# The first map's maximum of the next step moved ahead of this step's combination, in the differential-attention heads

## The chip, the cores and the metric

The kernel runs on one NeuronCore of a Trainium2 chip. The metric is the device time of one launch in microseconds. The engines named below are PE (TensorE, the matrix engine; PEld is its loading of weights), DVE (VectorE), ACT (ScalarE), POOL (GpSimd) and SP (the engine that issues most of the DMA). Each works through its own list of instructions in the order in which the program gives them, and they meet only at semaphores.

## What is computed

One layer of a streaming encoder runs for 512 prompt rows, 16 learned meta rows and 64 sample rows with a cache: a combined projection, two groups of attention heads, an output projection, and then a retrieval of single-row experts (PEER), which takes most of the time. The change touches only the first group of heads, A: four heads of differential attention. A head has two maps of scores over the same keys. Each map gets a softmax, and the second is subtracted with a factor lambda before the product with the values:

```python
s = jnp.einsum('bqhmd,bkhmd->bhmqk', q, kk).astype(jnp.float32) * (HEAD_DIM ** -0.5)
mask = (chunk_index(k_pos)[None, :] <= chunk_index(q_pos)[:, None]) & k_valid[None, :]
p = jax.nn.softmax(jnp.where(mask, s, NEG_BIG), axis=-1)
w = p[:, :, 0] - lam * p[:, :, 1]
return jnp.einsum('bhqk,bkhe->bqhe', w.astype(v.dtype), v)
```

Queries see all chunks of 64 keys up to their own, so a block of 128 queries needs fewer keys the earlier it stands.

## The kernel before

The A heads run between about 314 and 400 us of the execution, after the eight B heads and ahead of the head norms and the output projection. Nothing else runs on PE, ACT and DVE in that stretch, and POOL is idle. The work is cut into 20 steps, five for each of the four heads: four blocks of 128 prompt queries against 144, 272, 400 and 528 keys, then one block of 64 sample queries against 592 keys. The steps are named here by that width. A step does the following, and each part has a place in the list of its engine:

- PE, `a_scores` (L782 to L797): the scores of both maps. Map m (0 or 1) goes to its own pair of PSUM banks, 0 and 1 for the first map, 2 and 3 for the second. There is one set of them only, so the scores of a map wait until ACT has taken the exponentials of that map of the step before (L786). `a_s` counts them.
- DVE, `a_greatest` (L1458 to L1475): for each map a memset that masks a corner of the scores (L1468, L1469, L1471; none in the 592 step), the row maximum (L1472) and its negative times the scale (L1475, `a_neg`).
- ACT (L1094 to L1120): the exponential of each map with that number as bias, written to `p_a` with the row sums beside it (L1104, `a_prob`). Behind the two exponentials of step s stand the copy of the outputs of step s-2 (L1112) and the copies of the transposed weights of step s-1 to `wt_a` (L1118 and L1120).
- DVE, the combination (L1482 to L1490): when both maps of the step have come, two reciprocals of the sums (L1483), the product with lambda (L1484), and the two passes that give `w_a` (L1488 and L1489, `a_w`).
- PE, `a_transpose` (L799 to L809): the weights of the step, transposed tile by tile to banks 4 and 5 (L806 and L808). It waits for `a_w` of the step and for the copies of the step before.
- PE, `a_values` (L811 to L825): the product with the values (L824), once ACT has copied the transposed weights out.

PE's order is written out by hand: in iteration n it issues the scores of step n+1, then the values of step n-1, then the transposes of step n. So the scores of step n+1 stand behind the transposes of step n-1, and behind the values of step n-2. DVE's order is: both maxima of step 0; then for each step its combination, and behind it both maxima of the next step. The tile `stat` holds the maxima, the biases, the row sums and the reciprocals of one step, in columns 0 to 8 of 16.

Of the kernel before, what the change touches and what calls it, by code (L numbers as in the profile page):

```python
# [11 lines left out]
ALU = mybir.AluOpType  # L12
ACT = mybir.ActivationFunctionType
AX_X = mybir.AxisListType.X

P = 128
# [10 lines left out]
CHUNK = 64  # L27
EPS = 1e-6
LAM_INIT = 0.2
SCALE = HD ** -0.5  # L30
NEG = -1e30
# [121 lines left out]
NA = 5 * AH  # L153
# [11 lines left out]
def bass_hybrid_step(nc, x_t, consts, tables, gains, lam_p, cache_k, cache_v, cache_vt, w_tiles, sub_keys,  # L165
# [5 lines left out]
    with ExitStack() as ctx:  # L171
        base = [16512]

        def at(name, shape, dt, off):
            return nc.alloc_sbuf_tensor_at(name, shape, dt, offset=off)

        def fixed(name, shape, dt=F32):
            n = 4 * int(np.prod(shape[1:]))
            n = (n + 31) // 32 * 32
            off = base[0]  # L180
            base[0] += n
            return at(name, shape, dt, off)

        def sem(name):
            return ctx.enter_context(nc.semaphore(name))
# [6 lines left out]
        lam = fixed("lam", [P, 8])  # L192
        lam_in = fixed("lam_in", [P, 256])

        ones_r, tri_r, ident_r, negm_r = (fixed(n, [P, P], F32R) for n in ("ones_r", "tri_r", "ident_r", "negm_r"))
        stat = fixed("stat", [P, 16])
        rs_keep = fixed("rs_keep", [P, 8])
        raw_off = base[0]
        raw = fixed("raw", [P, 2, KC, P])
# [50 lines left out]
        p_a = at("p_a", [P, 4, T], F32, m0_off)  # L250
        w_a = at("w_a", [P, 2, T], F32, m0_off + 16 * T)
# [71 lines left out]
                  for k, o in enumerate((sc_off + 24576, sc_off + 30720, norm_off + 6 * T * 4 + 4608))]  # L323
# [7 lines left out]
        psf = ps[:].rearrange("p b n -> p (b n)")  # L331
# [17 lines left out]
                     for n, no in (("n1", "x"), ("nm", "added"), ("n2", "rs"))}  # L349
# [10 lines left out]
        a_s, a_max, a_neg, a_prob = sem("a_s"), sem("a_max"), sem("a_neg"), sem("a_prob")  # L360
        a_step, a_w, a_t, a_wt, a_o, a_out = (sem("a_step"), sem("a_w"), sem("a_t"), sem("a_wt"), sem("a_o"),
                                              sem("a_out"))
# [28 lines left out]
        MULT, ADD, SUB = ALU.mult, ALU.add, ALU.subtract  # L391
# [149 lines left out]
        def _(pool):  # L541
# [34 lines left out]
            for s, (table, blk, k) in enumerate(OPS):  # L576
                if s == 0:
                    pool.wait_ge(idx_ready, 1)
                if s == N_UA:
                    pool.wait_ge(idx_ready, 2)  # L580
                slot, _, before = ring_slots[s]
                if before is not None:
                    pool.wait_ge(gath_used, before + 1)
                if before is None and slot >= RING_U:
                    pool.wait_ge(u_done, N_EXP)
                idx = idx_b[:, k:k + 1] if blk else idx_a[:, k:k + 1]
                pool.indirect_dma_start(ring[slot][:], None, u_rows if table == "u" else v_rows,  # L587
                                        bass.IndirectOffsetOnAxis(ap=idx, axis=0)).then_inc(gath_in[slot], 16)
# [400 lines left out]
        def _(act):  # L989
# [38 lines left out]
            for m, o, n in ((P, 0, 4), (T - 4 * P, 4, 1)):  # L1028
                nc.scalar.activation(nrs1[0:m, o:o + n], ps[0:m, 4, o:o + n], ACT.Sqrt, bias=eps[0:m],
                                     scale=1.0 / D).then_inc(n1["std"], 1)  # L1030
            for n in range(2, N_QKV + 1):
# [9 lines left out]
                for h in range(2):  # L1041
                    for i in vt_after(n - 1, h):
                        kt, s = VT_GROUPS[i]
                        act.wait_ge(vt_done, i + 1)
                        rows = 128 if kt < 4 else 80
# [50 lines left out]
            for s in range(NA + 2):  # L1096
                if s < NA:
                    i = s % 5
                    rows, w = (P, 144 + P * i) if i < 4 else (64, T)
                    for m in range(2):  # L1100
                        act.wait_ge(a_neg, 2 * s + m + 1)
                        if s >= 2:
                            act.wait_ge(a_w, s - 1)
                        nc.scalar.activation(p_a[0:rows, 2 * (s % 2) + m, 0:w], psf[0:rows, 1024 * m:1024 * m + w],  # L1104
                                             ACT.Exp, bias=stat[0:rows, 2 + m:3 + m], scale=SCALE,
                                             accum_out=stat[0:rows, 4 + m:5 + m]).then_inc(a_prob, 1)
                if s >= 2:
                    h, i = (s - 2) // 5, (s - 2) % 5
                    rows = A_SHAPE[i][0]
                    q0 = N_META + P * i if i < 4 else KP  # L1110
                    act.wait_ge(a_o, s - 1)
                    nc.scalar.copy(qkv[:, 8 + h, q0:q0 + rows], ps[:, 6 + s % 2, 0:rows]).then_inc(a_out, 1)  # L1112
                if 1 <= s <= NA:
                    rows, full, part = A_SHAPE[(s - 1) % 5]
                    act.wait_ge(a_t, s)
                    if s >= 3:
                        act.wait_ge(a_o, s - 2)
                    nc.scalar.copy(wt_a[:, (s - 1) % 2, 0:full, 0:rows],  # L1118
                                   ps[:, 4, 0:full * rows].rearrange("p (k q) -> p k q", q=rows))
                    nc.scalar.copy(wt_a[0:part, (s - 1) % 2, full, 0:rows], ps[0:part, 5, 0:rows]).then_inc(a_wt, 1)  # L1120
# [11 lines left out]
            m = TQ - 4 * P  # L1132
# [28 lines left out]
            for u in range(N_PQ):  # L1161
                n = B_PQ + u
                hi_part(n + 1, (u + 1) % 2, (n + 1) // 2 + 1)
                for h in range(2):
# [4 lines left out]
                    if h == 0 and u == 0:  # L1169
                        act.wait_ge(norm_sems["n2"]["sum"], 1)  # L1170
                        nc.scalar.activation(nrs[:, 0:5], ps[:, 4, 0:5], ACT.Sqrt, bias=eps,
                                             scale=1.0 / D).then_inc(norm_sems["n2"]["std"], 1)
# [108 lines left out]
            for n, (b, m) in enumerate(FIN):  # L1281
                act.wait_ge(y_sum, n + 1)
                nc.scalar.activation(sq_out[0:m], h_fin[0:m, b], ACT.Square,
                                     accum_out=ss[0:m, n:n + 1]).then_inc(y_sq, 1)
                act.wait_ge(y_sq, n + 1)
                nc.scalar.activation(ss[0:m, 8 + n:9 + n], ss[0:m, n:n + 1], ACT.Sqrt, bias=eps[0:m],
                                     scale=1.0 / D).then_inc(y_std, 1)
# [3 lines left out]
        def _(dve):  # L1291
            TT, TS = nc.vector.tensor_tensor, nc.vector.tensor_scalar
# [159 lines left out]
            def a_step_done(ins):  # L1452
                nonlocal k_step
                ins.then_inc(a_step, 1)
                k_step += 1
                dve.wait_ge(a_step, k_step)

            def a_greatest(idx):  # L1458

                i = idx % 5  # L1460
                rows, w = (P, 144 + P * i) if i < 4 else (64, T)
                for m in range(2):
                    dve.wait_ge(a_s, 2 * idx + m + 1)
                    if i < 4:

                        e0 = 1024 * m + w
                        if w > 512 and w - CHUNK < 512:
                            nc.vector.memset(psf[0:CHUNK, e0 - CHUNK:1024 * m + 512], NEG)  # L1468
                            a_step_done(nc.vector.memset(psf[0:CHUNK, 1024 * m + 512:e0], NEG))  # L1469
                        else:  # L1470
                            a_step_done(nc.vector.memset(psf[0:CHUNK, e0 - CHUNK:e0], NEG))  # L1471
                    nc.vector.tensor_reduce(stat[0:rows, m:m + 1], psf[0:rows, 1024 * m:1024 * m + w], AX_X,  # L1472
                                            ALU.max).then_inc(a_max, 1)
                    dve.wait_ge(a_max, 2 * idx + m + 1)
                    TS(stat[0:rows, 2 + m:3 + m], stat[0:rows, m:m + 1], -SCALE, None, MULT).then_inc(a_neg, 1)  # L1475

            a_greatest(0)
            for idx in range(NA):
                i = idx % 5
                rows, w = (P, 144 + P * i) if i < 4 else (64, T)  # L1480
                p0 = 2 * (idx % 2)
                dve.wait_ge(a_prob, 2 * idx + 2)  # L1482
                a_step_done(nc.vector.reciprocal(stat[0:rows, 6:8], stat[0:rows, 4:6]))  # L1483
                TT(stat[0:rows, 8:9], stat[0:rows, 7:8], lam[0:rows, 5:6], MULT).then_inc(a_step, 1)  # L1484
                k_step += 1
                if idx >= 2:
                    dve.wait_ge(a_t, idx - 1)
                a_step_done(TS(w_a[0:rows, idx % 2, 0:w], p_a[0:rows, p0, 0:w], stat[0:rows, 6:7], None, MULT))  # L1488
                nc.vector.scalar_tensor_tensor(w_a[0:rows, idx % 2, 0:w], p_a[0:rows, p0 + 1, 0:w], stat[0:rows, 8:9],  # L1489
                                               w_a[0:rows, idx % 2, 0:w], MULT, ADD).then_inc(a_w, 1)  # L1490
                if idx + 1 < NA:
                    a_greatest(idx + 1)

            dve.wait_ge(a_t, 5 * AH)
            dve.wait_ge(a_o, 5 * AH)
# [233 lines left out]
            for i in range(N_EXP):  # L1729
# [9 lines left out]
                for _ in range(along(STEP_LINE, i), along(STEP_LINE, i + 1)):  # L1739
                    s = next(steps)  # L1740
# [173 lines left out]
```

## Time and profile before

| quantity | value |
| --- | --- |
| median of three runs | 1907.2 us (1906.71 to 1913.32) |
| the profiled execution's own time | 1903.46 us |
| its span in the trace | 1901.7 us |
| mean granted clock of PE, as a share of 2.4 GHz | 0.964 |
| busy over the span: PE, DVE, ACT, POOL | 95%, 75%, 40%, 34% |
| stretch of the A heads, first maximum to last combination | 315.05 to 396.4 us |

The page cuts the span in 40 slices of 47.5 us; the A heads lie in the seventh and eighth. The shares of busy time are means over all stages, and say little of one that is 4% of the span. A row of the timeline gives the start in the span, the time it took, the engine, the line and the operation, output and inputs with their sizes, and in brackets how long the engine had been idle and what ended that. Two PE instructions stand for each fp32 product, and the time of one reaches past the start of the next, so the distance between starts is the better measure on PE. The granted clock has two levels in these rows, 1.00 (2.4 GHz) and 0.50 (1.2 GHz).

### The profile page before, as it was taken

The numbers are of one execution on the slowest core, as the hardware profiler recorded it, in microseconds if no ns is written. First come the engines' busy times: TensorE is split into PE (matmuls) and PEld (weight loads), VectorE is DVE, ScalarE is ACT, GpSimd is POOL, SyncE is SP. The second block draws the span as 40 slices with busy tenths as digits, with TensorE's granted clock in tenths as the row PEclk, the third lists the DMA queues.
The fourth block names the chain that finished last, engine by engine and source line by source line (L and its number), as shares of the span: only waits on it lengthen the run. The fifth ranks groups of instructions, "written<-read, shape, count | busy, mean of one in ns | idle before, by whom it ended". The sixth has DMA issues, their size and how long they took to land.

```text
span 1901.7 us, 26560 instructions
## 1 busy us (share of the span) xinstructions
PE 1802.8 (95%) x9787; PEld 1543.1 (81%) x9787; DVE 1435.7 (75%) x2752; ACT 769.7 (40%) x1535; POOL 645.4 (34%) x409
## 2 busy tenths in 40 slices
PE   6999999999999889999899999978999999999997
PEld 6999666579999889999899999967766766766764
DVE  4433675735678788989999999858687788797787
ACT  4122564543444433433667788512222222222222
POOL 1200000000000033434233356545475566575662
PEclk9999898859999999999999999989999999999998
DMA  6243100002221589999788899999999999999996
GB/s 215 71 147 106 34 1 1 1 3 67 68 78 59 180 309 330 323 306 328 259 280 297 283 380 387 386 403 372 401 375 387 402 397 385 400 382 390 400 380 219
DMA packets 156480, 484.52 MB, mean 255 GB/s; under 512 B 15216, under 2 KB 56176, under 8 KB 152768
## 3 DMA queue, kind: packets, MB, share of 16 engines
q1 hardware_dynamic: 98992, 270.92, 39.1%
q0 software_dynamic: 56928, 208.28, 29.9%
q10 hardware_dynamic: 432, 3.64, 0.5%
q8 instruction: 78, 1.28, 0.3%
q14 instruction: 50, 0.41, 0.1%
HBM read 422.61 MB, written 59.90 MB: 254 GB/s over the span
## 4 chain that ended last, share of the span: by engine, by line
PE 66%; DVE 16%; DMA 12%; issue 3%; ACT 2%; SPq 0%; DVEq 0%; ACTq 0%
PE ps L973 16%; PE ps L951 15%; PE ps L607 10%; DMA g_in<-gates_scattered 7%; PE ps L982 5%; PE ps L888 5%; DVE hot L1690 3%; DVE w_lo L1296 3%; PE ps L708 3%; DMA raw<-w_tiles 2%; DVE ring L1709 2%; PE ps L939 2%; PE ps L699 2%; PE ps L751 2%; PE ps L795 1%
## 5 line engine op out<-in xcount | busy, mean ns | idle before, releaser
L951 PE MATMUL ps<-md_hi,w_hi 128*128 128x384 f32 x1024 | 360.8, 352 | 39.1 <-DVE w_lo L1296 39.0
L951 PE MATMUL ps<-md_hi,w_lo 128*128 128x384 f32 x1024 | 348.0, 340 | 0.0
L951 PE MATMUL ps<-md_lo,w_hi 128*128 128x384 f32 x1024 | 347.9, 340 | 0.0
L587 POOL DMA_INDIRECT ring<-u_rows,idx_a x128 | 197.0, 1539 | 402.6 <-DVE dots L1709 294.7
L1296 DVE TENSOR_TENSOR w_lo<-raw,w_hi 128x1024 fp32r<-128x1024 f32 x176 | 215.2, 1223 | 88.3 <-ACT w_hi L1226 68.0
L587 POOL DMA_INDIRECT ring<-v_rows,idx_a x128 | 223.8, 1749 | 139.1 <-DVE acc L1717 107.8
L1709 DVE CUSTOM_DVE_ANT_0 ring<-ring,x_n 128x1024 f32<-128x1024 f32 x192 | 230.3, 1221 | 10.6 <-DMA ring<-u_rows,idx_b 8.8
L951 PEld LDWEIGHTS ps<-md_hi,w_hi 128*128 128x128 f32 x1024 | 196.3, 192 | 47.2 <-DVE w_lo L1296 46.5
L1717 DVE SCALAR_TENSOR_TENSOR acc<-ring,actg,acc 128x1024 f32<-128x1024 f32 x188 | 234.1, 1277 | 0.0
L973 PE MATMUL ps<-w_hi,p_hi 128*128 128x512 f32 x576 | 192.0, 415 | 10.5 <-DVE w_lo L1773 10.3
L951 PEld LDWEIGHTS ps<-md_lo,w_hi 128*128 128x128 f32 x1024 | 196.4, 192 | 0.0
L951 PEld LDWEIGHTS ps<-md_hi,w_lo 128*128 128x128 f32 x1024 | 195.6, 191 | 0.0
L973 PE MATMUL ps<-w_hi,p_lo 128*128 128x512 f32 x576 | 182.3, 397 | 0.0
L973 PE MATMUL ps<-w_lo,p_hi 128*128 128x512 f32 x576 | 180.6, 395 | 0.0
L1265 ACT CAST w_hi<-v_buf 128x1024 fp32r<-128x1024 f32 x96 | 100.4, 1046 | 189.0 <-PE ps L973 176.4
L1773 DVE TENSOR_TENSOR w_lo<-v_buf,w_hi 128x1024 fp32r<-128x1024 f32 x96 | 117.1, 1220 | 77.8 <-ACT w_hi L1265 77.7
L607 PE MATMUL ps<-m_hi,w_hi 128*128 128x296 f32 (+1 forms) x512 | 157.0, 307 | 15.6 <-DVE w_lo L1296 14.8
L982 PE MATMUL ps<-v_buf,act_in 128*128 128x512 f32 x384 | 170.0, 592 | 0.0
L607 PE MATMUL ps<-m_hi,w_lo 128*128 128x296 f32 (+1 forms) x512 | 154.0, 301 | 0.0
L607 PE MATMUL ps<-m_lo,w_hi 128*128 128x296 f32 (+1 forms) x512 | 153.6, 300 | 0.0
L973 PEld LDWEIGHTS ps<-w_hi,p_hi 128*128 128x128 f32 x576 | 107.6, 189 | 52.9 <-issue 29.5
L1226 ACT CAST w_hi<-raw 128x1024 fp32r<-128x1024 f32 x127 | 132.4, 1042 | 35.6 <-DMA raw<-w_tiles 35.6
(254 smaller groups left out, 3269.8 us busy)
## 6 DMA issues: line engine op xcount, KB each, us to landing
raw<-w_tiles SPq DMA_DIRECT2D x176, 512.0 KB, 5.5
v_buf<-v_rows SPq DMA_DIRECT2D x128, 512.0 KB, 12.6
activated<-act_st SPq DMA_DIRECT2D x128, 192.0 KB, 4.7
gates_scattered<-g_st SPq DMA_DIRECT2D x24, 1024.0 KB, 6.4
g_in<-gates_scattered SPq DMA_DIRECT2D x32, 768.0 KB, 16.8
act_in<-activated SPq DMA_DIRECT2D x32, 768.0 KB, 13.7
kv_t<-qkv ACTq DMA_DIRECT2D x3, 1184.0 KB, 4.8
xh<-x_t SPq DMA_DIRECT2D x8, 296.0 KB, 6.2
```

The source lines that it names most:

```text
L587: pool.indirect_dma_start(ring[slot][:], None, u_rows if table == "u" else v_rows, bass.IndirectOffsetOnAxis(ap=idx, axis=0)).then_inc(gat ...
L607: mm = nc.tensor.matmul(ps[:, 2 * slot + h, 0:width], w[:, slot, kc, :], x[:, kc, c0:c0 + width], start=(m == 0), stop=(m == 23))
L888: mm = nc.tensor.matmul(ps[:, 2 * slot + h, 0:HQ], w[:, slot, kc, :], x[:, kc, h * HQ:(h + 1) * HQ], start=(kc == 0 and j == 0), stop=(kc ...
L951: mm = nc.tensor.matmul(ps[:, slot, 0:ND], w[:, slot, kc, :], x[:, kc, :], start=(kc == 0 and j == 0), stop=(kc == KC - 1 and j == 2))
L973: mm = nc.tensor.matmul(ps[:, 2 + 2 * t + h, :], p[:, q % 3, t * P:(t + 1) * P], v[q % 2][:, 512 * h:512 * h + 512], start=(i == 0 and n = ...
L982: mm = nc.tensor.matmul(ps[:, 2 + 2 * t + h, :], act_in[i // 4 % 3][:, i % 4, t * P:(t + 1) * P], v_buf[i % V_SLOTS][:, 512 * h:512 * h + ...
L1226: nc.scalar.copy(w_hi[:, n % 2], raw_u[k]).then_inc(hi_ready, 1)
L1265: nc.scalar.copy(v_hi[q % 2], v_buf[i % V_SLOTS][:]).then_inc(v_hi_ready, 1)
L1296: TT(w_lo[:, slot], raw[:, slot] if src is None else src, w_hi[:, slot].bitcast(F32), SUB).then_inc(w_split, 1)
L1709: nc.vector.tensor_tensor_reduce(rows, rows, x_n[:, blk], 1.0, 0.0, MULT, ADD, dots[:, blk, k:k + 1]).then_inc(gath_used, 1)
L1717: nc.vector.scalar_tensor_tensor(dst, rows, by, dst, MULT, ADD).then_inc(gath_used, 1)
L1773: TT(v_lo[q % 2], v_buf[i % V_SLOTS][:], v_hi[q % 2].bitcast(F32), SUB).then_inc(v_ready, 1)
```

## The change

DVE's `a_greatest` takes one map instead of both. In the new order the first map's maximum of step n+1 stands ahead of the combination of step n, and the second map's behind it. Since the numbers of step n are still needed when those of step n+1 are written, `stat` gets 32 columns, and step n uses columns 16 * (n % 2) onwards; ACT reads the bias and writes the sums there. No instruction is added or removed, no size is changed, and PE's order and ACT's order stay as they were.

```diff
-        stat = fixed("stat", [P, 16])
+        stat = fixed("stat", [P, 32])
...
+                    z = 16 * (s % 2)
...
-                                             ACT.Exp, bias=stat[0:rows, 2 + m:3 + m], scale=SCALE,
-                                             accum_out=stat[0:rows, 4 + m:5 + m]).then_inc(a_prob, 1)
+                                             ACT.Exp, bias=stat[0:rows, z + 2 + m:z + 3 + m], scale=SCALE,
+                                             accum_out=stat[0:rows, z + 4 + m:z + 5 + m]).then_inc(a_prob, 1)
...
-            def a_greatest(idx):
+            def a_greatest(idx, m):
...
-                for m in range(2):
-                    dve.wait_ge(a_s, 2 * idx + m + 1)
+                z = 16 * (idx % 2)
+                dve.wait_ge(a_s, 2 * idx + m + 1)
...
-            a_greatest(0)
+            a_greatest(0, 0)
+            a_greatest(0, 1)
             for idx in range(NA):
+                if idx + 1 < NA:
+                    a_greatest(idx + 1, 0)
...
                 dve.wait_ge(a_prob, 2 * idx + 2)
...
                 if idx + 1 < NA:
-                    a_greatest(idx + 1)
+                    a_greatest(idx + 1, 1)
```

## Rows read from the trace of the kernel before

**Rows 1.** The page: its span, and the engines of the chain that ended last.

```profile
span 1901.7 us, 26560 instructions
...
PE 66%; DVE 16%; DMA 12%; issue 3%; ACT 2%; SPq 0%; DVEq 0%; ACTq 0%
```

**Rows 2.** Stretches of the A heads: length; busy PE, PEld, DVE, ACT, POOL; granted clock; DMA.

```profile
315.05:396.40 81.35, 75.29 (x318) 46.38 (x319) 57.17 (x200) 38.44 (x136) 0.00 (x0) 0.75 0.00 1
317.70:331.36 13.66, 12.77 (x39) 7.18 (x39) 9.08 (x33) 5.74 (x20) 0.00 (x0) 0.50 0.01 2
331.36:345.01 13.65, 12.38 (x67) 7.81 (x65) 10.00 (x37) 7.38 (x28) 0.00 (x0) 1.00 0.00 0
345.01:351.84 6.83, 6.83 (x24) 3.91 (x23) 4.60 (x15) 2.39 (x8) 0.00 (x0) 0.50 0.00 0
351.84:365.50 13.66, 12.42 (x65) 7.76 (x65) 10.03 (x38) 7.41 (x28) 0.00 (x0) 1.00 0.01 1
365.50:372.32 6.82, 6.82 (x26) 4.29 (x25) 4.95 (x16) 2.41 (x8) 0.00 (x0) 0.50 0.00 1
...
379.14:392.80 13.66, 13.66 (x46) 8.14 (x45) 9.09 (x31) 5.84 (x21) 0.00 (x0) 0.50 0.01 2
```

**Rows 3.** Waits in 315 to 400 us: who for whom, total us, times, longest.

```profile
DVE stat L1483 <- ACT p_a L1104: 14.8, 20, 0.9
...
DVE stat L1472 <- PE ps L795: 3.0, 4, 1.1
DVE ps L1468 <- PE ps L795: 2.4, 2, 1.2
```

**Rows 4.** One head, 355.89 to 375.66 us: stretch, then DVE's groups by line.

```profile
355.89:375.66 19.77, 18.69 (x87) 11.67 (x86) 14.30 (x51) 9.77 (x35) 0.00 (x0) 0.83 0.01 1
...
L1472 DVE TENSOR_REDUCE stat<-ps 128x1 f32<-128x144 f32 (+4 forms) x10 | 5.6, 558 | 1.0 <-PE ps L795 0.8
...
L1483 DVE RECIPROCAL stat<-stat 128x2 f32<-128x2 f32 (+1 forms) x5 | 0.8, 164 | 3.7 <-ACT p_a L1104 3.7
```

**Rows 5.** Timeline of DVE: the maxima of steps 144 and 592.

```profile
355.89 0.11 DVE L1471 MEMSET ps<- 64x64 f32 x1
...
356.54 0.11 DVE L1471 MEMSET ps<- 64x64 f32 x1
...
371.29 0.77 DVE L1472 TENSOR_REDUCE stat<-ps 64x1 f32<-64x592 f32 x1 [0.77 <-PE ps L795]
...
372.16 0.76 DVE L1472 TENSOR_REDUCE stat<-ps 64x1 f32<-64x592 f32 x1
```

**Rows 6.** Timeline of PE at clock 1.00: first-map scores, and transposes of step 528.

```profile
357.10 0.72 PE L795 MATMUL ps<-qkv 64*128 64x272 f32 x2
...
360.13 0.94 PE L795 MATMUL ps<-qkv 64*128 64x400 f32 x2 [0.19 <-ACT p_a L1104]
...
372.99 0.42 PEld L806 LDWEIGHTS ps<-cst,w_a 128*128 128x128 f32 x4
...
373.69 0.51 PE L795 MATMUL ps<-qkv 64*128 64x144 f32 x2
```

**Rows 7.** Timeline at clock 0.50: scores of 528, transposes of 400, scores of 592.

```profile
384.58 2.33 PE L795 MATMUL ps<-qkv 64*128 64x512 f32 x8
...
388.70 0.50 PEld L806 LDWEIGHTS ps<-cst,w_a 128*128 128x128 f32 x3 [0.22 <-issue]
...
389.75 0.18 PEld L795 LDWEIGHTS ps<-k_cache,qkv 64*64 64x64 f32 x1 [0.42 <-issue]
...
392.02 0.77 DVE L1472 TENSOR_REDUCE stat<-ps 64x1 f32<-64x592 f32 x1 [0.52 <-PE ps L795]
```

**Rows 8.** Timeline: values of step 528 and the transposes behind them; ACT's first copy.

```profile
355.03 1.38 PEld L824 LDWEIGHTS ps<-wt_a,v_nat 128*128 128x128 f32 x10 [0.48 <-ACT wt_a L1120]
...
356.53 0.20 PEld L806 LDWEIGHTS ps<-cst,w_a 64*128 64x128 f32 x2
...
374.02 0.58 ACT L1118 COPY wt_a<-ps 128x512 f32<-128x512 f32 x1
```

More of the change, by code:

```diff
@@ L1456, in a_step_done @@
                 dve.wait_ge(a_step, k_step)
-            def a_greatest(idx):
+            def a_greatest(idx, m):
                 i = idx % 5
                 rows, w = (P, 144 + P * i) if i < 4 else (64, T)
-                for m in range(2):
-                    dve.wait_ge(a_s, 2 * idx + m + 1)
[L1464 to L1475, printed above, removed]
@@ L1477, in _ @@
-            a_greatest(0)
+                z = 16 * (idx % 2)
+                dve.wait_ge(a_s, 2 * idx + m + 1)
+                if i < 4:
+                    e0 = 1024 * m + w
+                    if w > 512 and w - CHUNK < 512:
+                        nc.vector.memset(psf[0:CHUNK, e0 - CHUNK:1024 * m + 512], NEG)
+                        a_step_done(nc.vector.memset(psf[0:CHUNK, 1024 * m + 512:e0], NEG))
+                    else:
+                        a_step_done(nc.vector.memset(psf[0:CHUNK, e0 - CHUNK:e0], NEG))
@@ L1478, in _ @@
+                nc.vector.tensor_reduce(stat[0:rows, z + m:z + m + 1], psf[0:rows, 1024 * m:1024 * m + w], AX_X,
+                                        ALU.max).then_inc(a_max, 1)
+                dve.wait_ge(a_max, 2 * idx + m + 1)
+                TS(stat[0:rows, z + 2 + m:z + 3 + m], stat[0:rows, z + m:z + m + 1], -SCALE, None, MULT).then_inc(a_neg, 1)
+            a_greatest(0, 0)
+            a_greatest(0, 1)
             for idx in range(NA):
+                if idx + 1 < NA:
+                    a_greatest(idx + 1, 0)
@@ L1479, in _ @@
                 i = idx % 5
                 rows, w = (P, 144 + P * i) if i < 4 else (64, T)
-                p0 = 2 * (idx % 2)
+                p0, z = 2 * (idx % 2), 16 * (idx % 2)
                 dve.wait_ge(a_prob, 2 * idx + 2)
-                a_step_done(nc.vector.reciprocal(stat[0:rows, 6:8], stat[0:rows, 4:6]))
-                TT(stat[0:rows, 8:9], stat[0:rows, 7:8], lam[0:rows, 5:6], MULT).then_inc(a_step, 1)
+                a_step_done(nc.vector.reciprocal(stat[0:rows, z + 6:z + 8], stat[0:rows, z + 4:z + 6]))
@@ L1485, in _ @@
+                TT(stat[0:rows, z + 8:z + 9], stat[0:rows, z + 7:z + 8], lam[0:rows, 5:6], MULT).then_inc(a_step, 1)
                 k_step += 1
@@ L1487, in _ @@
                     dve.wait_ge(a_t, idx - 1)
-                a_step_done(TS(w_a[0:rows, idx % 2, 0:w], p_a[0:rows, p0, 0:w], stat[0:rows, 6:7], None, MULT))
-                nc.vector.scalar_tensor_tensor(w_a[0:rows, idx % 2, 0:w], p_a[0:rows, p0 + 1, 0:w], stat[0:rows, 8:9],
+                a_step_done(TS(w_a[0:rows, idx % 2, 0:w], p_a[0:rows, p0, 0:w], stat[0:rows, z + 6:z + 7], None, MULT))
+                nc.vector.scalar_tensor_tensor(w_a[0:rows, idx % 2, 0:w], p_a[0:rows, p0 + 1, 0:w], stat[0:rows, z + 8:z + 9],
                                                w_a[0:rows, idx % 2, 0:w], MULT, ADD).then_inc(a_w, 1)
                 if idx + 1 < NA:
-                    a_greatest(idx + 1)
+                    a_greatest(idx + 1, 1)
             dve.wait_ge(a_t, 5 * AH)
```

## The prediction

> **What bounds the kernel now.** I read the page first: the chain that ended last lies 66% on PE and 16% on DVE [rows 1], but that is a mean over the whole kernel. So the second view is the table of stretches of the A heads [rows 2], the third who waited for whom there [rows 3], the fourth DVE's groups in one head [rows 4]. The stage from first maximum to last combination takes 81.35 us. Two things are to be seen. DVE is busy 57.2 of 81.35 us. And PE is at its lower clock level, 0.50 (1.2 GHz), in four stretches: 13.66 + 6.83 + 6.82 + 13.66 = 41.0 us, half of the stage; outside them it is at 1.00 (2.4 GHz) [rows 2]. DVE waits 14.8 us, in 20 waits, for the exponentials (one at each combination) and 3.0 + 2.4 = 5.4 us, in 6 waits, for scores [rows 3]; the first of these two is what the change aims at. Every wait of the second kind that I found lies where the clock is 0.50 or was so when the scores were made; the two in rows here (0.77 and 0.52 us) do [rows 5, 7].
>
> So DVE bounds the stage nearly alone. A head is a loop of five steps on DVE: both maxima, the wait for the second exponential, the combination. Head three shows it: 19.77 us, of which 3.7 wait for exponentials and 0.8 for scores; the other 15.27 are work with its hand-offs (14.30 busy) [rows 4]. In this I need the maxima apart. From the start of one map's maximum to the start of the next map's it is 0.65 us at 144 keys (355.89 to 356.54) and 0.87 at 592 (371.29 to 372.16) [rows 5], the first and last of five; the three between read the same way give 0.78, 0.91 and 1.05, longest at 528, which has two memsets. One map of a head costs 0.65 + 0.78 + 0.91 + 1.05 + 0.87 = 4.26 us, the combinations 15.27 - 2 x 4.26 = 6.75.
>
> **The change, part by part.** No instruction comes or goes and no size changes, and no DMA issue is moved; SP and POOL have nothing in this part of their lists that hangs on it. The wider `stat` costs 64 bytes a partition and no time. The second set of columns takes away a dependency only. Both are costed at nothing, with no cover needed.
>
> What is left is the order on DVE. Before, from the end of one combination to the start of the next, DVE does maximum, maximum, wait for an exponential. Per head that is 2 x 4.26 + 3.7 = 12.2, plus score waits. After, it does the second maximum of step n, then the first maximum of step n+1, and only then the combination of n. The exponential of the second map now runs beside that first maximum: 0.65 to 1.05 us of cover for waits of 14.8 / 20 = 0.74 on average. That wait goes, nearly whole: 3.7 us a head.
>
> The price: the moved maximum waits for `a_s` of step n+1, and the combination of step n is queued behind that wait, with the copies, the values and the transposes that hang on it. In PE's list the first-map scores of step n+1 stand behind the transposes of step n-1, which wait for the combination of n-1. Before, this path had the whole of two maxima and an exponential to hide in. Now DVE's loop goes through it: end of combination n-1, transposes of n-1, first-map scores of n+1, first maximum of n+1, combination of n. In each step DVE's time between combination n-1 and the moved maximum is the larger of one maximum and the PE path. What the change trades, per head, is
>
> - gone: one map's maxima from the line between combinations, 4.26, and the exposed exponentials, 3.7: 7.96 us at either clock; and the score waits, 5.4 / 4 = 1.35 on average;
> - in: the PE path, five times.
>
> The path at clock 1.00. Transposes to scores: 0.70 for five tiles (372.99 to 373.69); four loads took 0.42, so 0.105 a tile and 0.17 after the last [rows 6]. By that the transposes of 144, 272, 400, 528 take 0.38, 0.49, 0.59, 0.70, and those of 592, five half-size tiles, I put at 0.48: sum 2.64. First-map scores: 0.51 for 144 keys, 0.72 for 272, 0.94 for 400 [rows 6]; with 0.04 to reach DVE 0.55, 0.76, 0.98. The wider ones don't stand alone in the trace at this clock; I take half of the clock-0.50 durations below plus a fixed 0.1: 1.27 and 1.24. Sum 4.80. Hand-offs from DVE to PE: 5 x 0.04 = 0.2. Once a head PE comes late to the transposes: at the 592 step the values of 528 take 1.50 (355.03 to 356.53) [rows 8] and start only when ACT has done its second exponential and the copies; laid out along the new order they end 0.5 after the combination. Sum 2.64 + 4.80 + 0.2 + 0.5 = 8.1 us. Against 7.96 that is even: a head of 15.27 - 4.26 + 8.1 = 19.1 us, where one without score waits took 15.27 + 3.7 = 18.97.
>
> The path at clock 0.50. Four tiles and the gap behind them take 1.05 (388.70 to 389.75); first-map scores of 592 reach DVE after 2.27 (389.75 to 392.02); those of 528 take 2.33 from 384.58, both maps side by side, so one is hardly shorter [rows 7]. Scaled by tiles and by keys: transposes 0.63, 0.83, 1.05, 1.27, 0.79, sum 4.6; scores 0.90, 1.32, 1.75, 2.34, 2.28, sum 8.6. With 0.2 of hand-offs and PE late by 0.9 in two or three places, 14.3 us. A head: 11.0 + 14.3 = 25.3 us. The heads before, half at this level, took 20.3 each on average (81.35 / 4).
>
> These are the ends, 8.1 and 14.3; the share of each clock decides between them. I take the share that the stage has now, one half of the time: heads per us are 0.5 / 19.1 + 0.5 / 25.3, so a head takes 21.8 us and four take 87.1. That is 87.1 - 81.35 = 5.7 us more. The gain (3.7 a head) is there and is used up, because work that hid under DVE's loop is now a link of it. What is late next is PE: the transposes and scores.
>
> A rule of the Trainium skill speaks to that share. The rows show PE's clock rising behind stretches in which it never stood still: at 351.84 behind 6.83 us in which PE was busy for 6.83, at 372.32 behind 6.82 of 6.82 [rows 2]. "TensorE: Matmul & The Clock Gate", part 1, says that the throttled state is the default and that activity releases it, and the trace agrees. Taken strictly, a stage in which PE's waits get shorter would keep the higher level, which is the third rival below; by the share of now it is the sum above.
>
> **The sum.** The profiled execution took 1903.46 us, span 1901.7; with 5.7 more it would take 1909.2. The median of the three runs, 1907.2, is 3.7 above that execution, so I add the same 5.7 to it: 1912.9, given as 1913.
>
> **Rivals.**
> 1. The low clock holds longer. PE has more to wait for in each loop at 0.50, and if the level sticks, DVE's loop is PE's: slower. For: the two long low stretches (13.66 us) show that it can stay for more than half a head [rows 2]. Against: at 0.50 the new loop keeps PE almost without a gap, after which it rose each time. At a share of 65% four heads take 4 / (0.35 / 19.1 + 0.65 / 25.3) = 90.8, 9.5 over now; all low is 101.2, 19.9 over. From about 65% on it decides: 1917 to 1927 us.
> 2. The path is hidden after all: PE gets the scores done under the second maximum, or my chain has a link that isn't there. Then DVE loses only its waits for exponentials, 14.8 us, and keeps the 5.4 for scores: 1907.2 - 14.8 = 1892.4. Against: PE's written order leaves no way for scores n+1 to pass transposes n-1, and even at 1.00 the path of every step (1.3 us or more) is longer than a maximum (0.65 to 1.05).
> 3. The clock stays at 1.00 nearly throughout. Four heads of 19.1 are 76.4, 4.9 less than now: 1902.3; with up to a third of the time low, up to 1909. For: the rule above. Against: the stage has fallen back to 0.50 four times while PE was busy 12.4 of 13.65 us [rows 2], and the new order doesn't make it much denser.
> 4. The change does nothing, because the order makes no difference. It can't be quite so: DVE takes its list in order, so the combination does stand behind the new wait. A net of zero is possible, inside case 3.
>
> **How the numbers follow.** Forecast 0.67 (share of the low clock a third to 65%; 1909 to 1917), rival 1 0.17 (1917 to 1927), rival 3 with 4 0.13 (1902 to 1909), rival 2 0.03. The likeliest is 1913. The range reaches over most of rival 3 and the nearer half of rival 1, leaving out rival 2 and the far ends: 1903 to 1921. 0.5%, about what a measurement of this kernel can tell from no change, is 9.5 us: faster means under 1897.7, slower above 1916.7. Faster 0.03 (rival 2); slower 0.20 (rival 1 and the edge of the forecast); within 0.77.
>
> **What the profile of the changed kernel would show.** The waits of L1483 for exponentials fall from 14.8 us to under 2. DVE's waits for L795 rise from 5.4 us to 20 or more, in nearly all of 19 steps, and are longest ahead of the maxima of 528 and 592. The chain in this stretch alternates L806, L795, L1472, L1489. Busy times of DVE and ACT stay. A head takes about 19 us where the clock is 1.00 and 24 to 25 where it is 0.50. The prediction is wrong if L1472's waits for L795 stay near 5 us (rival 2), or if the low level holds for well over or under half of the stage (rivals 1 and 3).

## The result, and the profile after

| quantity | before | after |
| --- | --- | --- |
| median | 1907.72 us (12 runs, 1898.06 to 1917.91) | 1921.65 us (12 runs, 1917.36 to 1931.96) |
| ratio | | 1.0074, 95% interval 1.0053 to 1.0096 |
| profiled execution: own time, span | 1903.46, 1901.7 us | 1919.99, 1918.2 us |
| A heads, first maximum to last combination | 315.05 to 396.4, 81.35 us | 317.0 to 414.4, 97.4 us |

The change is slower by 14 us, 0.74%. In the profiled executions it is 16.5 us of span, and 16.1 of them lie in the A heads; from the last combination to the end it is 1505.3 us before and 1503.8 after. So the place is settled without an experiment: the rest of the kernel is as it was, within 2 us on either side.

A single execution of either kernel can still differ from another by more than the change does. One source lies ahead of the A heads, in a part that no run here touches: in the profiled executions the A heads start between 314.9 us and 327.1 us. In the three that start at 326 us or later (the experiments e1, e6 and e8 below) the clock was low for longer in the B heads. The stretch from 200 to 250 us, in the kernel before (mean clock 0.83) and in e6 (0.56):

```profile
200.00:250.00 50.00, 48.77 (x265) 35.48 (x266) 36.02 (x91) 30.64 (x72) 0.00 (x0) 0.83 0.00 1
200.00:250.00 50.00, 49.19 (x189) 34.74 (x189) 26.48 (x66) 22.69 (x54) 0.00 (x0) 0.56 0.00 1
```

So the length of the A heads, read from a profile, says more about this change than one execution's total does.

The stretches of the A heads after the change (as [rows 2]: length; busy PE, PEld, DVE, ACT, POOL; granted clock; DMA). The first block is the page's span. In the second block the first line is the stage, the second its longest stretch at one clock level, the third one head.

```profile
span 1918.2 us, 26560 instructions
```

```profile
317.00:414.40 97.40, 93.44 (x315) 59.99 (x316) 55.34 (x199) 38.40 (x136) 0.00 (x0) 0.53 0.00 1
319.80:391.50 71.70, 70.19 (x234) 45.70 (x234) 39.65 (x143) 28.11 (x99) 0.00 (x0) 0.50 0.00 1
344.72:370.03 25.31, 24.94 (x87) 16.47 (x86) 13.84 (x52) 9.80 (x36) 0.00 (x0) 0.50 0.00 1
```

DVE's busy time is nearly what it was (57.2 and 55.3 us; in the rows below each reciprocal starts while the small instruction ahead of it still runs, 349.12 against 349.05 + 0.15), and so is ACT's. What changed is the clock: 0.53 on average over the stage, against 0.75 in [rows 2]. A mean of 0.53 from two levels means 94% of the time at 0.50. PE shows busy 70.19 of 71.70 us in the low stretch, and the level did not rise within it.

Who waited for whom on DVE, 317 to 415 us (us in total, times, longest), against [rows 3]. The lines of the changed kernel are numbered a little differently: the reciprocal is L1487, a map's masking starts at L1469 or L1472, and its maximum is L1473.

```profile
DVE ps L1472 <- PE ps L795: 17.9, 11, 2.1
DVE stat L1473 <- PE ps L795: 9.8, 4, 2.5
DVE ps L1469 <- PE ps L795: 9.5, 4, 2.4
DVE stat L1487 <- ACT p_a L1105: 0.9, 1, 0.9
```

The waits for exponentials are gone, 14.8 us down to 0.9, the one that is left being that of the last step. In their place stand 37.2 us of waits for scores, in 19 waits, one for each moved maximum, where there were 5.4 us in 6. The timeline of DVE over one step shows the new order:

```profile
349.05 0.15 DVE L1476 TENSOR_SCALAR stat<-stat 128x1 f32<-128x1 f32 x1
349.12 0.16 DVE L1487 RECIPROCAL stat<-stat 128x2 f32<-128x2 f32 x1
...
349.78 0.50 DVE L1493 SCALAR_TENSOR_TENSOR w_a<-p_a,stat,w_a 128x272 f32<-128x272 f32 x1
350.29 0.11 DVE L1472 MEMSET ps<- 64x64 f32 x1
...
351.04 0.15 DVE L1476 TENSOR_SCALAR stat<-stat 128x1 f32<-128x1 f32 x1
353.56 0.10 DVE L1469 MEMSET ps<- 64x48 f32 x1 [2.37 <-PE ps L795]
```

The combination of the 272 step runs without a wait (349.12), then comes the second maximum of the 400 step (350.29), and then DVE stands 2.37 us for the first-map scores of the 528 step. Over the five steps of this head the waits are 2.13, 2.37, 2.46, 1.79 and 1.73 us. The chain of waits shows what they wait for (start, length, what):

```profile
349.78 0.51 DVE w_a L1493
350.30 0.04 issue
350.34 0.69 PE ps L806 x2
351.03 0.21 PE ps L808
351.24 2.24 PE ps L795 x5
353.48 0.36 issue
353.84 0.45 PE ps L795 x2
354.28 1.87 PE ps L824 x6
356.15 0.83 PE ps L806 x3
356.99 0.21 PE ps L808
357.20 2.16 PE ps L795 x5
```

From the end of a combination it goes to the transposes and to the scores, as the new loop has it; and on the wide steps it doesn't come back to DVE at all, but runs through scores, values (L824) and transposes on PE alone. At this clock PE is the bound for most of the head. The rows of PE say the same: in four of the five steps the transposes start 0.2 to 0.57 us after the combination is done, because PE is still at the values of the step before; only at the 272 step (done at 350.28, started at 350.34) is PE ready.

### The profile page after: what moved, and what is told of

Same layout as the page of the kernel before. It is cut to its first block, busy times and chain, and to the rows that moved or that the text cites. A ratio compares the mean times of both kernels' runs of the same rounds, so it can differ in the third digit from the quotient of the medians.

```text
span 1918.2 us, 26560 instructions
## 1 busy us (share of the span) xinstructions
PE 1824.1 (95%) x9787; PEld 1558.5 (81%) x9787; DVE 1434.5 (75%) x2752; ACT 770.2 (40%) x1535; POOL 645.4 (34%) x409
## 4 chain that ended last, share of the span: by engine, by line
PE 72%; DVE 16%; DMA 7%; ACT 3%; issue 2%; SPq 0%; DVEq 0%; ACTq 0%
PE ps L973 18%; PE ps L951 16%; PE ps L607 10%; PE ps L982 7%; PE ps L888 5%; DMA g_in<-gates_scattered 3%; DVE w_lo L1297 3%; DVE hot L1694 3%; PE ps L708 3%; DVE ring L1713 2%; DMA raw<-w_tiles 2%; PE ps L939 2%; PE ps L795 2%; PE ps L824 2%; PE ps L699 2%
```

## The experiments

Two theories stood after the result. One: the new order costs what the sum says, and the excess over 5.7 us is the clock, which stayed at 0.50. The other: something else of the change costs (the wider tile), or the path is longer than summed even at clock 1.00. Medians and ratios are over all executions, the ratios against runs of the kernel before on the same chip. The last two columns are each from the one profiled execution of the run; "low" is the share of clock 0.50 in the A heads of the run's profile, worked out from the granted clock as in the section above.

| run | median us | ratio, 95% interval | A heads us | low |
| --- | --- | --- | --- | --- |
| the changed kernel | 1921.65 | 1.0074 (1.0053 to 1.0096) | 97.4 | 94% |
| e1_stat_only | 1904.69 | 0.9987 (0.9964 to 1.0011) | 81.8 | 58% |
| e2_scores_ahead | 1943.64 | 1.0182 (1.0119 to 1.0245) | 116.4 | 97% |
| e3_scores_ahead_old_dve | 1945.47 | 1.0188 (1.0136 to 1.024) | 117.2 | 98% |
| e5_start_together | 1933.0 | 1.0138 (1.0078 to 1.0198) | 103.8 | 90% |
| e6_after_fill | 1912.88 | 1.0039 (1.0005 to 1.0073) | 85.2 | 12% |
| e7_before_fill | 1903.57 | 0.9987 (0.9958 to 1.0015) | 78.5 | 13% |
| e8_ahead_fill | 1982.06 | 1.0375 (1.0323 to 1.0427) | 148.3 | 98% |
| e9_after_fill_early | 1919.42 | 1.0078 (1.0051 to 1.0105) | 98.9 | 72% |
| e10_only_144_fill | 1930.14 | 1.0135 (1.0108 to 1.0163) | 93.9 | 73% |
| e11_before_fill_early | 1911.29 | 1.0013 (0.9989 to 1.0036) | 82.6 | 43% |
| e12_before_fill_again | 1905.05 | 0.9989 (0.997 to 1.0008) | 78.4 | 13% |
| e4_after_again (one execution) | 1919.63 | | 94.7 | 86% |

**The wider tile alone.** DVE's old order in the changed kernel:

```diff
             for idx in range(NA):
-                if idx + 1 < NA:
-                    a_greatest(idx + 1, 0)
...
                 if idx + 1 < NA:
+                    a_greatest(idx + 1, 0)
                     a_greatest(idx + 1, 1)
```

> The changed kernel with DVE's old order put back: both maxima of the next step behind the combination. What stays of the change is the wider stat with its two sets of columns. Theory (the new order costs the time, through the path transposes, first-map scores, first maximum): like the kernel before, ratio 0.997 to 1.003, DVE's waits for L795 about 5 us in the A heads, for exponentials about 15. Rival (the wider tile, which moves every later tile by 64 bytes, or the alternating columns, cost something): a good part of the 14 us stays, ratio 1.004 or more.

It measures as the kernel before, 0.9987 with an interval around 1. Its A heads:

```profile
326.10:407.90 81.80, 76.87 (x318) 48.48 (x319) 57.07 (x199) 38.39 (x136) 0.00 (x0) 0.71 0.00 1
```

81.8 us at a mean clock of 0.71. The tile costs nothing that can be measured here; the 14 us are the order. The share of the low clock is 58% in this profile and was 50% in the kernel before, with the same order of work: it moves by that much between two executions.

**First-map scores ahead of the transposes.** If the loop through the transposes is the cost, it can be cut in PE's list:

```diff
             a_scores(0)
+            a_scores(1, (0,))
             for idx in range(NA + 1):
                 if idx + 1 < NA:
-                    a_scores(idx + 1)
+                    a_scores(idx + 1, (1,))
                 if idx >= 1:
                     a_values(idx - 1)
+                if idx + 2 < NA:
+                    a_scores(idx + 2, (0,))
```

e2 has it on the changed kernel, e3 on the kernel before.

> The changed kernel with PE's list changed too: the first-map scores of step n+2 stand ahead of the transposes of step n (and behind the values of n-1), so that the moved maximum no longer waits for transposes. Theory: the loop through the combination, the transposes and the scores is cut; DVE's waits for L795 fall well under the changed kernel's. At clock 1.00 a head should take about 17.5 us instead of 19.1, the stage about 73 us, 8 less than before: 1900 us. At clock 0.50 the two maps' scores no longer run side by side and PE alone needs about 30 us a head, so a stage that stays low would take up to 120 us and the kernel would be slower than the changed one, 1935 or more. Rival (the moved maximum itself, not its wait on PE's order, costs the time): like the changed kernel, 1921, at any clock.

> The kernel before, with the same change of PE's list and DVE's old order. Theory: at clock 1.00 nothing changes, because DVE's loop of two maxima, an exponential and a combination (19 us a head) doesn't go through the scores: 1907. At clock 0.50 the scores of the two maps are apart, PE needs 30 us a head, and the stage can take 120 us: up to 1945. So this run tells what the place of the first-map scores does by itself, and with the run of both changes beside it, what DVE's order does when PE doesn't hold it up: 6 us less at clock 1.00.

```profile
318.40:434.80 116.40, 114.33 (x311) 65.54 (x311) 55.68 (x199) 39.14 (x134) 0.00 (x0) 0.51 0.00 1
```

```profile
315.80:433.00 117.20, 114.29 (x311) 65.55 (x311) 57.47 (x200) 39.19 (x134) 0.00 (x0) 0.51 0.00 1
```

The first line is e2, the second e3. Both took the bad branch of their expectation: the clock stayed at 0.50 for 97 and 98% of the stage, PE alone is the bound (busy 114 of 116 and of 117 us), a head takes 30.5 us in both, and DVE's order makes no difference any more. The two maps' scores read different halves of the partitions (64 each). In the kernel before, at clock 0.50, they ran side by side: the 528 step's eight products took 2.33 us in all [rows 7]. With one map moved away they run one after the other, and in e3 the four products of one map take nearly as long as the eight did:

```profile
355.78 2.31 PE L795 MATMUL ps<-qkv 64*128 64x512 f32 x4
```

So these runs don't tell what the moved maximum does where PE is free. They do show two things: a PE that its rows show busy 98% of the time can stay at the lower level for over 100 us (114 in e2, 115 in e3), and it can do so with DVE's old order too.

**Starting both maps together again.** That suggested that the side-by-side scores are what brings the clock up, and that the change had taken them apart: in its low stretch the eight products of the 528 step take 3.11 us (from 351.17), those of the 592 step 2.92 (from 357.13), where 2.33 and 2.43 stood before. Changed kernel, 528 step:

```profile
351.17 3.11 PE L795 MATMUL ps<-qkv 64*128 64x512 f32 x8
```

```diff
-                        pe.wait_ge(a_prob, 2 * idx - 1 + m)
+                        pe.wait_ge(a_prob, 2 * idx if i >= 3 else 2 * idx - 1 + m)
```

> The changed kernel, but in the 528 and 592 steps PE lets the first map's scores wait until the second map's exponential of the step before is done too, so that both maps' scores start side by side, as they did in the kernel before at the low clock. Theory A (the share of the low clock, 95% of the stage in the changed kernel's profile against 50% before, follows from PE no longer running both maps' widest scores side by side): the clock rises again behind the 592 steps, the share falls to near one half, and the stage falls from 98 us towards 88, 1912 in all, although each such step waits up to 0.6 us longer. Theory B (the share has nothing to do with that): the share stays above 85%, and the time is that of the changed kernel or up to 5 us more, 1921 to 1927.

Theory A fell. The low share is 90%, the stage 103.8 us, the kernel 1933, slower than either of its expectations. The timeline has the 592 step's scores side by side, eight products in 2.25 us:

```profile
361.22 2.25 PE L795 MATMUL ps<-k_cache,qkv 64*64 64x512 f32 x8 [0.76 <-ACT p_a L1105]
```

The clock stayed down behind most of them, and the extra wait is simply on DVE's loop: a head takes 26.6 us.

**Extra work on PE.** The direct test of the clock is to give PE more to do without changing any order:

```diff
+            def a_fill(idx):
+                if idx >= 2:
+                    pe.wait_ge(a_out, idx - 1)
+                for _ in range(8):
+                    nc.tensor.matmul(ps[:, 6 + idx % 2, 0:P], ones_r[:], tri_r[:], start=True, stop=True)
...
                 if idx < NA:
+                    a_fill(idx)
                     a_transpose(idx)
```

> The changed kernel with eight extra 128-column products a step (constants times constants, into the output bank that is free, overwritten by the values that follow), put into PE's list ahead of the transposes, where PE often waits for the combination. They add work and remove none: 0.43 us a step at clock 1.00, 0.85 at clock 0.50. Theory A (the loss of the change is mostly the low clock, which holds because PE is seldom dense in the new loop): the share of the low clock in the A heads falls from 94% to about half or less, a head takes about 20 us for most of the stage, the stage falls from 97 to 80 to 88 us and the kernel to 1905 to 1912. Theory B (the clock isn't to be moved by such work, or isn't what costs): the extra work only lengthens PE's part, 20 x 0.85 less what lies in waits, 5 to 15 us slower than the changed kernel.

> The kernel before with the same eight products a step. Theory A: the clock is at 1.00 for most of the A heads, the DVE loop of 19 us a head hides the extra work, the stage goes from 81 to 77 to 80 us: 1903 to 1907. Theory B: 0 to 10 us slower than the kernel before, as the extra work comes on the low stretches where PE is the later.

The A heads of e6, a head of it, the A heads of e7 and a head of it:

```profile
326.90:412.10 85.20, 81.85 (x470) 57.21 (x471) 55.33 (x199) 38.32 (x136) 0.00 (x0) 0.94 0.00 1
340.88:361.25 20.37, 20.03 (x123) 14.30 (x123) 13.84 (x51) 9.67 (x35) 0.00 (x0) 1.00 0.00 0
```

```profile
315.40:393.90 78.50, 75.56 (x470) 55.67 (x471) 56.73 (x200) 38.84 (x136) 0.00 (x0) 0.93 0.00 1
338.97:357.90 18.93, 18.61 (x127) 13.99 (x127) 14.21 (x50) 9.89 (x36) 0.00 (x0) 1.00 0.00 1
```

160 products more, nothing less, and the stage of the changed kernel gets 12 us shorter (97.4 to 85.2), its mean clock goes from 0.53 to 0.94. The median falls from 1921.65 to 1912.88, just over the 1905 to 1912 that was expected. These two medians come from different sets of runs: each against the kernel before in its own set, the loss is 13.9 us without the extra work and 8.3 with it, and the two intervals of the ratio overlap, so for the whole kernel the gain is likely but not shown. That the clock moved does not hang on one profile: the mean granted clock of a whole execution is 0.958 to 0.971 in all ten executions of e6, and 0.944 to 0.953 in all twelve of the changed kernel. At nearly the same clock the two orders are 6.7 us apart in the stage (85.2 and 78.5), where they were 16.1 apart. So the larger part of the loss in the A heads went with the clock, and the clock can be moved by what PE is given. The kernel before, with the same work, has its stage at 78.5 us and heads of 18.93 us at clock 1.00, where the sum had 18.97 for a head without score waits.

At the same clock the order still costs: heads of 20.4 to 20.8 us in e6 against 18.93. Part of that is the extra work itself, as the timeline of e6 shows:

```profile
357.56 1.11 PE L832 MATMUL ps<-tri_r,ones_r 128*128 128x128 f32 x8
358.50 0.41 PE L806 MATMUL ps<-cst,w_a 128*128 128x128 f32 x2
...
358.95 2.23 PE L795 MATMUL ps<-qkv 64*128 64x512 f32 x8
```

```profile
357.74 0.50 DVE L1500 SCALAR_TENSOR_TENSOR w_a<-p_a,stat,w_a 128x272 f32<-128x272 f32 x1
358.25 0.11 DVE L1479 MEMSET ps<- 64x64 f32 x1
```

The eight took 0.94 us (357.56 to 358.50; I had reckoned 0.43), and the transposes started at 358.50, not at 358.25 when the combination was done. In the new order that lies on DVE's loop; in the old it is hidden, since the head of e7 is no longer than the sum's.

**Both orders changed, with the extra work.**

> Both orders changed (first map's maximum ahead of the combination on DVE, first map's scores ahead of the transposes on PE), with the same eight products a step. Theory A: at clock 1.00 a head needs about 17.5 us of DVE's loop and 17 of PE's work, so the stage takes 73 to 78 us and the kernel 1898 to 1904, under both. Theory B: the clock stays low as without the extra work (97% of 116 us) and PE, the bound there, gets 17 us more: 1955 to 1965.

Theory A fell here: 98% low, 148.3 us for the A heads, 39.5 us a head. With the maps' scores apart even this much work leaves the clock down. Theory B was too low as well (1955 to 1965 expected, 1982 measured): the 40 extra products of a head cost 9.0 us of it (39.5 against 30.5 in e2), some 0.2 us each at clock 0.50 on the engine that is the bound.

**The order at clock 1.00.** To see the new order there without extra work in its path, four products stand between the scores and the values instead (e9); e11 is the kernel before with the same four, and e10 moves the maximum only where the next step is the 144 one.

> The changed kernel with four extra 128-column products a step, now between the scores and the values, where PE waits for ACT's copies, instead of ahead of the transposes, where the run with eight took 1.1 us a step and pushed the transposes back by some 0.3. Theory (at clock 1.00 the moved maximum is an even trade, as the sum had it): where the clock is 1.00 a head takes 19.0 to 19.5 us, against 20.7 with the eight. If the clock holds at 1.00 the stage takes 77 to 80 us and the kernel 1903 to 1906, as the one before. Rival (the order costs at clock 1.00 too): 20 us a head or more at 1.00. Four may be too few to move the clock: then heads of 25 to 26 us and 1922.

> The kernel before with the same four products a step between scores and values. Theory: 18.9 to 19.0 us a head at clock 1.00, since DVE's loop hides PE; the share of the low clock lower than the 50% of the kernel before; 1902 to 1907. It is the measure for the two runs beside it.

> As the run beside it, but the first maximum is moved only where the next step is the 144 one, which is the one place where the sum for clock 1.00 has a gain (path and maximum 1.9 us against 2.7 for maximum, maximum and exponential of the 592 step); in the other steps DVE keeps its old order. Theory: 18.2 to 18.5 us a head at clock 1.00, 0.6 under the run without the move; in the kernel's time 2 us, not to be told from nothing. If the path is longer than summed, 19 or more a head.

With four, at this other place, the clock did not hold in e9: 72% low, and in that part heads of 27.75 us (25 to 26 were expected). But the last 24 us of its stage run at 1.00. A head's length of e9 there, the same starting a step later (the two overlap, so they are one piece of evidence), and a head of e11:

```profile
391.67:410.66 18.99, 17.86 (x99) 11.73 (x99) 13.84 (x51) 9.55 (x35) 0.00 (x0) 1.00 0.00 1
395.13:413.98 18.85, 18.56 (x107) 12.63 (x107) 13.35 (x49) 9.41 (x35) 0.00 (x0) 1.00 0.00 1
```

```profile
340.06:358.97 18.91, 18.64 (x107) 12.50 (x105) 14.21 (x50) 9.65 (x36) 0.00 (x0) 1.00 0.00 1
```

At clock 1.00 the changed order takes 18.85 to 18.99 us a head and the old one 18.91: the even trade of the sum (19.1 and 18.97). The rival of 20 us or more does not fit this stretch, which is the only whole head that the changed order ran at 1.00 with no extra work ahead of the transposes.

e11 kept its expectation for the head and for the clock (43% low, under the 50% of the kernel before), but not for the time: 1902 to 1907 was expected, 1911.29 is its median. Its ratio, 1.0013 with an interval around 1, doesn't tell it from the kernel before, and its stage of 82.6 us is no shorter.

e10 missed its expectation: its heads took 23.9 us with 73% of the time low, and no head of it ran at 1.00 throughout, so what the single move is worth there stays open. Its profiled execution, at 1916.63 us, is the fastest of five; the other four took 1930.04 to 1933.92, so the stage behind the median of 1930.14 was not seen.

**Two repeats.**

> The changed kernel unaltered, a second profile. Theory (its own loop keeps PE at the low clock): the share of clock 0.50 in the A heads is again over 85%, with heads of 25.3 us where it holds throughout. Rival (the 94% of the first profile was chance, and the share swings between executions): a share near half, and then a time near 1912.

> The kernel before with eight extra products a step ahead of the transposes, once more and in more rounds, as the one version that might be under both kernels. By its heads (18.93 us at clock 1.00, stage 78.5 us against 81.2) it should gain 3 us in the A heads: ratio 0.998, between 0.996 and 1.000. If it isn't under 1.000 with its interval, nothing here beats the kernel before clearly.

The second profile of the changed kernel is low for 86% of the A heads. The stage, and a head of it:

```profile
320.40:415.10 94.70, 90.64 (x314) 57.44 (x315) 55.27 (x199) 38.18 (x136) 0.00 (x0) 0.57 0.00 1
343.13:367.07 23.94, 23.62 (x87) 15.27 (x87) 13.86 (x52) 9.70 (x35) 0.00 (x0) 0.57 0.00 0
```

The head takes 23.94 us at a mean of 0.57, which is 20.5 us at clock 0.50 and 3.4 at 1.00, and the other heads do the same. The two ends of the sum give 20.5 / 25.3 + 3.4 / 19.1 = 0.99 of a head for that. e12 is 0.9989 with an interval up to 1.0008: the kernel before with extra work may be 2 us better, but it isn't shown, and no kernel here is clearly under the kernel before. Its stage repeats that of e7: 78.4 us, 13% low.

## Why the prediction was wrong

The forecast was 5.7 us more, 1913, with a range to 1921; measured were 14 us more, 1921.65. The sign is right, the size is not. Point by point:

- "That wait goes, nearly whole: 3.7 us a head." Right: 14.8 us to 0.9.
- The new loop of DVE through transposes and first-map scores. Right: the chain of waits and 19 score waits show it; I had said 20 us of waits or more, and it was 37.2.
- The path at clock 1.00, 8.1 us against 7.96, a head of 19.1. Right: 18.85 to 18.99 in e9.
- The path at clock 0.50, 14.3 us, a head of 25.3. Right: 25.31 in the head shown above. The five waits of that head sum to 10.5 us, with one map's maxima (4.26) 14.7. The transposes measured 4.3 us (4.6 in the sum) and the scores 8.7 (8.6). How late PE came was underrated, 1.8 us over the five steps where the sum has 1.1 with its hand-offs; it had "PE late by 0.9 in two or three places" but added 0.9 only once. The rest of DVE's loop, 10.6 us instead of 11.0, made up for most of that, so the closeness of 25.3 is in part luck.
- "I take the share that the stage has now, one half of the time." This step failed. The share was 94% in one profile and 86% in the other. Put into the same formula, 94% gives 4 / (0.06 / 19.1 + 0.94 / 25.3) = 99 us for the stage, 86% gives 97; measured were 97.4 and 94.7. So the mechanism and both prices held within 2 us of the stage, and the term that decides between them was off: of the 16.1 us in the profiled stage, 5.7 are the order at the old share by the sum, and the rest, some 10, comes with the clock.

Behind that step was a treatment of the clock as a property of the stage, something that the change would find as it left it. The runs show it to be an outcome: the same order has 94% and 12% (the changed kernel without and with extra work), and 50% and 13% (the one before). Rival 1 described the case, with the point (65%) and the price (9.5 to 19.9 us), but at a chance of 0.17. My reason against it was that at 0.50 the new loop keeps PE almost without a gap, after which the clock had risen each time [rows 2]. That reason is refuted by a row: PE busy 70.19 of 71.70 us, at 0.50 throughout. What I took for the sign in the stretches ahead of each rise, a busy share of 1, is there for tens of us with no rise. It was a weak sign in [rows 2] already: PE was busy for the whole of the stretch from 379.14 to 392.80, and the level stayed at 0.50 for 13.66 us, twice as long as in the two stretches that I had read it from. Against rival 3 I misread the same rows: of the four falls to 0.50 only two, at 345.01 and 365.50, stand behind a stretch with some 12.4 of 13.65 us busy.

The rule of the Trainium skill ("TensorE: Matmul & The Clock Gate", part 1), that activity releases the throttle, agrees with e6 and e7, where more work brought the clock up; in e8 the same extra work did not. A busy share read from the rows can't be put in the place of that activity, as e2 and e3 show with 98% at the lower level. Rival 3, which rested on the rule, did not come.

What stays open is why the clock holds at 0.50 in the new loop. Side-by-side scores were in every stretch of the kernel before that ended in a rise, and e5, which brought them back in the 528 and 592 steps only, did not restore it; e8 shows that extra work is not enough where they are apart. That a slower loop (25 us a head instead of 20) spreads PE's work over more time and so keeps its own clock down is a guess; no run here tests it. e6 and e9 differ in how many extra products they have and in where these stand, so they don't tell which of the two counts.

## What to carry to other kernels

Before moving a wait up in an in-order list, follow what it waits for back through the other engine's list. Here the exposed 3.7 us a head were traded for a path through PE that had been free as long as it was hidden, an even trade at full clock. And where a stage swings between two clock levels, don't keep the share of the old profile: cost both levels, and don't give the low one a small chance when the change puts the clocked engine on the path. Here that chance was 0.17, and the low level took 94% of the stage.

## What the hardware showed that I had not expected

- The lower level held for 71.7 us on end while PE's rows were busy 98% of the time, and for 114 and 115 us in e2 and e3.
- 160 small products that compute nothing useful took 12 us off the A heads of the changed kernel and raised their mean clock from 0.53 to 0.94 (e6). Eight a step did it; four a step, at another place in PE's list, left e9 low for 72%.
- A 128-column product with its own load of weights took 0.12 us at clock 1.00 (eight in 0.94, e6), where I had reckoned 0.05 from its columns, and some 0.2 us at clock 0.50 (e8 against e2).
